# Depthwise-convolution taps taken off GpSimd, a new fold of the layer norm's squares, and a last residual add shared by four engines

## The reference

```python
def conformer_conv(h, w_pw1, b_pw1, w_dw, b_dw, ln_g, ln_b, w_pw2, b_pw2):
    u = h @ w_pw1 + b_pw1
    a, gate = jnp.split(u, 2, axis=-1)
    u = a * jax.nn.sigmoid(gate)
    u = lax.conv_general_dilated(u, w_dw[:, None, :], ...) + b_dw
    u = jax.nn.silu(layer_norm(u, ln_g, ln_b))  
    return u @ w_pw2 + b_pw2
```

## Time and profile before

| | us |
|---|---|
| median of 3 runs (lowest to highest) | 1835.67 (1832.31 to 1838.24) |
| the profiled execution's own time | 1825.88 |
| its span in the trace | 1824.1 |
| busy: TensorE, VectorE, ScalarE, GpSimd | 1770.6, 992.7, 632.3, 232.5 |

### The profile page before, as it was taken

One profiled execution on the slowest core, in us unless ns is written; L12 is line 12 of the kernel. 1 busy time (PEld: TensorE's weight loads), 2 busy tenths in 40 slices (PEclk: granted clock), 3 DMA queues, 4 the chain that ended last, 5 costly groups with the idle time before them and its releaser, 6 DMA issues.

```text
span 1824.1 us, 22032 instructions
## 1 busy us (share of the span) xinstructions
PE 1770.6 (97%) x8104; PEld 1438.0 (79%) x8104; DVE 992.7 (54%) x1299; ACT 632.3 (35%) x928; POOL 232.5 (13%) x200
## 2 busy tenths in 40 slices
PE   6999999999999999999999999999999999999997
PEld 5777888888888887867888888877767788888885
DVE  4566346663665389974743244336675564234423
ACT  4345234441344353343422123234264433113220
POOL 2100021110111122311110011000000111002111
PEclk9999899999999999989999999999999999999998
DMA  5212023333223222312133223321210223323221
GB/s 183 83 47 71 22 94 100 99 117 96 91 92 104 70 93 83 106 66 89 63 104 103 92 93 102 95 92 48 95 43 1 93 81 103 95 92 101 92 81 46
DMA packets 43844, 156.05 MB, mean 86 GB/s; under 512 B 4864, under 2 KB 4992, under 8 KB 43776
## 3 DMA queue, kind: packets, MB, share of 16 engines
q1 hardware_dynamic: 43632, 154.19, 26.3%
q10 hardware_dynamic: 144, 0.92, 0.1%
HBM read 153.00 MB, written 2.10 MB: 85 GB/s over the span
## 4 chain that ended last, share of the span: by engine, by line
PE 85%; DVE 11%; ACT 2%; issue 1%; POOL 0%; DMA 0%; POOLq 0%; SPq 0%; ACTq 0%; DVEq 0%
PE bank L1037 25%; PE bank L1038 24%; PE bank L1039 24%; DVE cv L1998 4%; DVE w_lo L1683 2%; PE bank L1172 1%; PE bank L1178 1%; PE bank L1173 1%; PE bank L1078 1%; PE bank L1248 1%; PE bank L1114 1%; PE bank L1277 1%; PE bank L1624 1%; ACT w_hi L622 1%; PE bank L1104 0%
## 5 line engine op out<-in xcount | busy, mean ns | idle before, releaser
L1683 DVE TENSOR_TENSOR w_lo<-w_raw,w_hi 128x1024 fp32r<-128x1024 f32 x283 | 367.9, 1301 | 319.3 <-ACT w_hi L622 196.5
L1037 PE MATMUL bank<-a_hi,w_hi 128*128 128x512 f32 x1156 | 460.4, 398 | 22.7 <-DVE w_lo L1683 20.1
L1038 PE MATMUL bank<-a_lo,w_hi 128*128 128x512 f32 x1156 | 455.4, 394 | 0.0
L1039 PE MATMUL bank<-a_hi,w_lo 128*128 128x512 f32 x1156 | 453.5, 392 | 0.0
L1037 PEld LDWEIGHTS bank<-a_hi,w_hi 128*128 128x128 f32 x1156 | 218.6, 189 | 77.5 <-issue 15.3
L1037 PE MATMUL bank<-g_hi,w_hi 128*128 128x512 f32 x688 | 270.1, 393 | 0.0
L1038 PE MATMUL bank<-g_lo,w_hi 128*128 128x512 f32 x688 | 270.0, 392 | 0.0
L1039 PE MATMUL bank<-g_hi,w_lo 128*128 128x512 f32 x688 | 267.7, 389 | 0.0
L1039 PEld LDWEIGHTS bank<-a_hi,w_lo 128*128 128x128 f32 x1156 | 218.4, 189 | 49.3
L1038 PEld LDWEIGHTS bank<-a_lo,w_hi 128*128 128x128 f32 x1156 | 218.8, 189 | 46.0 <-issue 1.0
L622 ACT ACTIVATE w_hi<-w_raw 128x1024 fp32r<-128x1024 f32 x167 | 173.9, 1049 | 174.1 <-PE bank L1039 168.9
(11 more groups left out here) (290 smaller groups left out, 2042.8 us busy)
## 6 DMA issues: line engine op xcount, KB each, us to landing
w_raw<-in_stream SPq DMA_DIRECT2D x283, 512.0 KB, 3.5
h<-in_xT SPq DMA_DIRECT2D x8, 256.0 KB, 6.7
out<-h SPq DMA_DIRECT2D x8, 256.0 KB, 2.0
cst_b<-in_consts SPq DMA_DIRECT2D x1, 896.0 KB, 9.7
cst_b<-in_consts ACTq DMA_DIRECT2D x1, 896.0 KB, 4.6
cols<-in_vectors SPq DMA_DIRECT2D x1, 289.0 KB, 2.8
cst<-in_consts SPq DMA_DIRECT2D x1, 257.0 KB, 8.3
w_al<-in_w_alpha SPq DMA_DIRECT2D x1, 128.0 KB, 9.9
```

The costliest lines, as they stand in the source:

```text
L1037: pe.matmul(out, w0, x0, start=start, stop=False, skip_group_check=loose)
L1038: pe.matmul(out, w0, x1, start=False, stop=False, skip_group_check=loose)
L1039: return pe.matmul(out, w1, x0, start=False, stop=stop, skip_group_check=loose)
L1683: dve.tensor_tensor(w_lo[slot][:, :], w_raw[slot][:, :], f(w_hi[slot][:, :]), ALU.subtract)\
```

## The change

`TAPS_PE` becomes `[12, 12, 12, 20]` and `TAPS_POOL` goes away, with its ScalarE products and its GpSimd adds; VectorE has 18, 18, 18 and 10 taps per tile, 128 in all. The tap units become 3, 3, 3 and 5. `w_hi` and `w_lo` of `pw2`'s units 2 and 3 are made ahead of the mean, behind the last tap addition. The layer norm's squares go into `m`; GpSimd adds two pairs, VectorE folds the other four tiles to one, and TensorE sums three tiles instead of four. The idle matmuls are laid differently: two before the mean instead of four, four behind it instead of two, others of 192, 512 and 256 columns between and behind the sums, and one instead of four behind the spread. In the last residual add VectorE does tiles 0 and 7, GpSimd 1, 3 and 5, and for tiles 2, 4 and 6 TensorE adds `h` and `m` in a bank by identity matmuls and ScalarE copies the bank to `h`; `h`'s own part is loaded into the banks in place of idle matmuls and behind the spread.

```diff
-TAPS_PE = [12, 12, 16, 16]
-TAPS_POOL = [2, 2, 3, 4]
+TAPS_PE = [12, 12, 12, 20]
...
+        def out_bank(k):
+            return bank[{2: 2, 4: 3, 6: 5}[k]]
...
@block.sync
             for k in range(KD):
-                sp.wait_ge(out_added if k % 2 else out_ready, k // 2 + 1)
+                if k in (2, 4, 6):
+                    sp.wait_ge(out_copied, k // 2)
+                elif k in (1, 3, 5):
+                    sp.wait_ge(out_added, k // 2 + 1)
+                else:
+                    sp.wait_ge(out_ready, 1 if k == 0 else 2)
                 sp.dma_start(outT[k * P:(k + 1) * P, :], T(h, k)).then_inc(out_stored, 16)
...
@block.gpsimd
-            def add_taps(k):
-                pool.wait_ge(last_tap, k + 1)
-                for j in range(TAPS_POOL[k // 2]):
-                    no = pool_taps(k) + j
-                    pool.wait_ge(tap_product, no + 1)
-                    if j:
-                        pool.wait_ge(pool_tap, no)
-                    pool.tensor_tensor(T(cv, k), T(cv, k), sq_buf[no % 2], ALU.add).then_inc(pool_tap, 1)
...
-                add_taps(2 * p)
-                add_taps(2 * p + 1)
...
-            for p in range(KD // 2):
+            for p in range(2):
                 pool.wait_ge(sq_ready, SQ0["ln_var"] + 2 * p + 2)
-                pool.tensor_tensor(ln_sq_buf(2 * p), ln_sq_buf(2 * p), ln_sq_buf(2 * p + 1), ALU.add)\
-                    .then_inc(sum_added, 1)
+                pool.tensor_tensor(T(m, 2 * p), T(m, 2 * p), T(m, 2 * p + 1), ALU.add).then_inc(ln_pairs, 1)
...
-            for k in range(1, KD, 2):
-                pool.wait_ge(out_scaled, (k + 1) // 2)
+            for k in (1, 3, 5):
+                pool.wait_ge(out_scaled, k)
                 pool.tensor_tensor(T(h, k), T(h, k), T(m, k), ALU.add).then_inc(out_added, 1)
...
@block.scalar
-                for j in range(TAPS_POOL[k // 2]):
-                    tap = CONV_W - 2 - j
-                    no = pool_taps(k) + j
-                    if no >= 2:
-                        act.wait_ge(pool_tap, no - 1)
-                    act.activation(sq_buf[no % 2], u_pad[:, k * UW + tap:k * UW + tap + SEQ], ACT.Copy,
-                                   scale=col("w_dw", k * CONV_W + tap)).then_inc(tap_product, 1)
...
+            w_hi_of(UNIT0["pw2"] + AHEAD, (UNIT0["pw2"] + AHEAD) % RING)
             load_sqrt(STAT_NO["ln_var"])
             act.wait_ge(mean_done, 1)
             for k in range(KD):
                 act.wait_ge(cen_ready, k + 1)
-                act.activation(ln_sq_buf(k), T(cv, k), ACT.Square, scale=float(D) ** -0.5).then_inc(sq_ready, 1)
-            w_hi_of(UNIT0["pw2"] + AHEAD, (UNIT0["pw2"] + AHEAD) % RING)
+                act.activation(T(m, k), T(cv, k), ACT.Square, scale=float(D) ** -0.5).then_inc(sq_ready, 1)
...
             feed_forward(1)
+            for k in (2, 4, 6):
+                act.wait_ge(out_summed, k // 2)
+                act.activation(T(h, k), out_bank(k)[:, :], ACT.Copy).then_inc(out_copied, 1)
...
@block.tensor
+            def h_part(k, c0, c1):
+                pe.matmul(out_bank(k)[:, c0:c1], cst[:, IDENT:IDENT + P], T(h, k)[:, c0:c1], start=(c0 == 0), stop=False,
+                          skip_group_check=True)
...
@@ in stat
-                if "post" in name:
+                if name == "ffpost1":
+                    pe.wait_ge(out_read, TILE0["ff2b1"])
+                    h_part(2, 0, 384)
+                elif "post" in name:
                     run_idle(6, 1, 384)
...
@@ in spread
+                if name == "ffpost1":
+                    h_part(4, 0, 384)
+                elif "post" in name:
                     run_idle(6, 1, 384)
...
             pe.wait_ge(out_read, TILE0["pw2"])
-            run_idle(0, 4)
+            run_idle(0, 2)
             pe.wait_ge(mean_add, KD - 2)
             pe.matmul(bank[4][:, :], cst[:, MEAN:MEAN + P], ssum[:, :], start=True, stop=False)
-            pe.wait_ge(cv_ready, KD)
-            pe.matmul(bank[4][:, :], cst[:, MEAN:MEAN + P], T(cv, KD - 2), start=False, stop=False)
-            pe.matmul(bank[4][:, :], cst[:, MEAN:MEAN + P], T(cv, KD - 1), start=False, stop=True)\
-                .then_inc(mean_done, 1)
+            for k in (KD - 2, KD - 1):
+                pe.wait_ge(cv_ready, k + 1)
+                last = pe.matmul(bank[4][:, :], cst[:, MEAN:MEAN + P], T(cv, k), start=False, stop=(k == KD - 1))
+            last.then_inc(mean_done, 1)
             run_idle(0, 2)
-            for p in range(KD // 2):
-                if p:
-                    run_idle(0, 1, P)
-                pe.wait_ge(sum_added, ADD0["ln_var"] + p + 1)
...
+            run_idle(0, 2)
...
+            pe.wait_ge(ln_pairs, 1)
+            ln_sum(0, True, False)
+            run_idle(0, 1, 192)
+            pe.wait_ge(ln_pairs, 2)
+            ln_sum(2, False, False)
+            run_idle(0, 1)
+            pe.wait_ge(ln_folded, 1)
+            ln_sum(4, False, True).then_inc(stat_done, 1)
+            run_idle(0, 1, 256)
             spread("ln_var")
-            run_idle(0, 4)
+            run_idle(0, 1)
             tiles("pw2", 8, a_hi, a_lo, "conv")
...
             feed_forward(1)
+            h_part(2, 384, SEQ)
+            h_part(4, 384, SEQ)
+            h_part(6, 0, SEQ)
+            run_idle(6, 1)
+            for k in (2, 4, 6):
+                pe.wait_ge(out_scaled, k)
+                pe.matmul(out_bank(k)[:, :], cst[:, IDENT:IDENT + P], T(m, k), start=False, stop=True,
+                          skip_group_check=True).then_inc(out_summed, 1)
...
@block.vector
-                return CONV_W - 1 - TAPS_POOL[p] - TAPS_PE[p]
+                return CONV_W - 1 - TAPS_PE[p]
...
-                        dve.wait_ge(pool_tap, pool_taps(c + 1))
+                        dve.wait_ge(last_tap, c + 1)
...
             add_pe_taps(KD // 2 - 1)
+            lo_ahead(UNIT0["pw2"] - 1)
+            lo_ahead(UNIT0["pw2"])
             dve.wait_ge(mean_done, 1)
             for k in range(KD):
                 dve.tensor_tensor(T(cv, k), T(cv, k), bank[4][:, :], ALU.subtract).then_inc(cen_ready, 1)
-            lo_ahead(UNIT0["pw2"])
+            for k, other in ((4, 5), (6, 7), (4, 6)):
+                dve.wait_ge(sq_ready, SQ0["ln_var"] + max(k, other) + 1)
+                fold = dve.tensor_tensor(T(m, k), T(m, k), T(m, other), ALU.add)
...
-            post_norm("ffpost1", "ffpost", 8, None)
+            take_r("ffpost1")
+            dve.wait_ge(spread_done, STAT_NO["ffpost1"] + 1)
+            for k in range(KD):
+                scale = dve.scalar_tensor_tensor(T(m, k), T(m, k), col("ffpost", 8 + k), bank[4][:, :],
+                                                 ALU.mult, ALU.mult)
+                if k in (0, KD - 1):
+                    link(scale)
+                    dve.tensor_tensor(T(h, k), T(h, k), T(m, k), ALU.add).then_inc(out_ready, 1)
+                else:
+                    scale.then_inc(out_scaled, 1)
```

More of the change, by code:

```diff
@@ L110 @@
     _s = _s + _n
-    if _name not in IN_M:
-        _a += max(_n - 2, 0) if _name != "ln_var" else KD // 2
+    if _name not in IN_M and _name != "ln_var":
+        _a += max(_n - 2, 0)
 R_NO = {name: i for i, name in enumerate(n for n, _ in STATS if "post" not in n and n != "ln_var")}
@@ L366, in program @@
         ln_silu = sem("ln_silu")
+        ln_pairs = sem("ln_pairs")
+        ln_folded = sem("ln_folded")
         h_ready = sem("h_ready")
@@ L444, in conv_step @@
             return first, taps
-        def pool_taps(c):
-            return sum(TAPS_POOL[k // 2] for k in range(c))
         def conv_bank(c):
@@ L2012, in _ @@
                 for q, n in enumerate(units):
-                    if n > UNIT0["pw1"]:
+                    if UNIT0["pw1"] < n < UNIT0["pw2"] - 1:
                         lo_ahead(n)
@@ L2038, in _ @@
                 dve.tensor_tensor(T(cv, k), T(cv, k), bank[4][:, :], ALU.subtract).then_inc(cen_ready, 1)
-            lo_ahead(UNIT0["pw2"])
+            for k, other in ((4, 5), (6, 7), (4, 6)):
+                dve.wait_ge(sq_ready, SQ0["ln_var"] + max(k, other) + 1)
+                fold = dve.tensor_tensor(T(m, k), T(m, k), T(m, other), ALU.add)
+                if other == 6:
+                    fold.then_inc(ln_folded, 1)
+                else:
+                    link(fold)
             take_r("ln_var")
@@ L2054, in _, with post_norm @@
                 dve.tensor_scalar(T(m, k), bank[k % 4][:, :], col("b_pw2", k), None, ALU.add).then_inc(out_read, 1)
-            def post_norm(stat, gain, g0, h0=None, split=None, next_gain=None, ng0=0, product=None):
+            def post_norm(stat, gain, g0, split, next_gain, ng0, product=None):
                 take_r(stat)
@@ L2065, in post_norm @@
                                                      ALU.mult, ALU.mult)
-                    if not split and k % 2:
-                        scale.then_inc(out_scaled, 1)
-                        continue
                     link(scale)
```

(9 more changed lines are left out.)

22 lines of the change are left out of this document (10 added, 12 removed).

## The result

The changed kernel's median is 1814.74 us (1813.4 to 1816.22, four runs) beside 1833.99 us for the kernel before (four runs): a ratio of 0.9895, 95% interval 0.9871 to 0.9919. So the kernel is 0.9 to 1.0% faster, 16 to 19 us. Forecast were 16.0 us (0.9913).

The account below looks back on a forecast made before the run. It took TensorE to bound the kernel, winnable only in waits, idle matmuls and low clock; gains of 7.0, 2.9, 2.9 and 3.2 us made 16.0: 1809.9 us profiled, 1819.7 timed, range 1814 to 1827.

Parts of the forecast that it names:

- Taps: Convolution: VectorE's end of taps moves from 794.5 to 785.8 us, TensorE's last unit from 790.6 to 786.2.
- The stretch: Convolution: 18 removed GpSimd adds lay beside VectorE's taps and what follows, costing it 1.04 us each, 18.7 in all.
- the two stalls and the low clock: Convolution: TensorE's two waits for w_lo, 2.7 us, and the half clock behind them, 1.7, together 4.4.
- Mean: Layer norm: the mean's last matmul ends (time M) at 790.9 us instead of 797.85, gain 7.0.
- Variance: Layer norm: scaling starts 9.8 us behind M, the end of the mean's last matmul, instead of 12.7; gain 2.9.
- The first rival: Layer norm: the clock falls all the same, costing 3.4 to 5.1 us, time 1823 to 1825; chance 20%.
- A clock of 0.5 around 795 us: Layer norm: a granted clock this low there was named as a sign that the forecast is wrong.
- First matmul of pw2: Behind the norm: one idle matmul instead of four frees TensorE in time for the first product, gain taken as 2.9 us.
- The end: Last residual add: the span ends 10.4 us behind T, the last norm's first scale, instead of 13.6; gain 3.2.
- VectorE starving TensorE: Convolution: TensorE still waits once for VectorE, so 4.4 us of wait and low clock stay, 1824 us; chance 12%.
- The folds: Variance: VectorE's folds meet GpSimd's second pair and lose 0.5 us, 1820.2, or up to 1.27, 1821; chance 5%.
- The slower side: Convolution: the stretch isn't GpSimd's doing and VectorE becomes the bound, 8.8 us slower, 1844.5 us; chance 3%.

Follow-up runs that it names:

- e7: The changed kernel with 22 GpSimd adds on unused spare tiles put back at the old tap adds' places: 1839.7 us, one run.
- e3: The kernel before with only the change's end part, the last residual add shared by four engines: ratio 1.0006 to the kernel before.
- e12: The changed kernel without idle matmuls before the mean, one w_lo moved into VectorE's wait for the spread, 192 idle columns widened to 448: 1811.97 us, ratio 0.9902.
- e5: The changed kernel again, unedited, against more runs of the kernel before: 1814.37 us beside 1831.0, ratio 0.9914.
- the first profile: The first profiled execution of the changed kernel, unedited: 1813.4 us, span 1811.6 us.
- e2: The kernel before with only the change's layer norm part: ratio 0.9983 to the kernel before.
- e9: The changed kernel with TensorE's old tap shares, TAPS_PE [12, 12, 16, 16]: ratio 0.9940 to the kernel before.
- e10: The changed kernel with four idle matmuls instead of one behind the layer norm's spread: ratio 0.9942 to the kernel before.
- e6: The changed kernel with the old end, VectorE adding even tiles and GpSimd odd ones: 1818.4 us, ratio 0.9932 to the kernel before.
- e8: The changed kernel with 22 spare GpSimd memsets, which read nothing, at the old tap adds' places: 1815.1 us, one run.
- e1: The kernel before with only the change's convolution part, 128 taps on VectorE and none on GpSimd: ratio 0.9975 to the kernel before.
- e4: The kernel before again, unedited: profiled execution 1829.74 us, median of runs 1830.97 us, ratio 1.0009 to the kernel before.

## Why the prediction was right, point by point

*What bounds the stage.* Right: VectorE's stretched taps held up w_lo, and with GpSimd's tap adds gone nothing waits for it. With adds on spare tiles back in their place (e7) it waits again.

*Taps.* Forecast for VectorE's end of taps 785.8, measured 785.3; the sum's terms stand nearly. The stretch was put at 18.7. In e7 it is 18.7 again, but that is not the same sum tap for tap: in the kernel before 14 of the 18 adds lie beside taps and stretch them by 1.04 each, the others mostly stretch u_lo and w_lo. The 1.2 us that VectorE idled for ScalarE's w_hi between 654 and 794.5 and that went away too were not counted. The early start of the first step was taken at 3.5 and came to 3.4 (650.97 for 654.33). Forecast for TensorE's last unit 786.2, measured 785.7: the two stalls and the low clock were worth 4.9, not 4.4; by e3, the low clock's 1.7 of it could have been missing before.

*Mean.* Forecast 790.9, measured 790.2. The two idle matmuls were counted as on the path. e12 shows that 1.5 of their 1.7 us are, once the second w_lo is out of the way as well.

*Variance.* Forecast M + 9.8 at full clock: 10.0 in e5, 11.8 in the first profile. The first rival, given 20%, is what happened in that profile: 6.8 us of low clock from 796.8. With the same idle work ahead of the spread the clock was low in that profile, e2, e7, e9 and e10, and up in e5, e6 and e8. Five of eight is far from 20%: the chance of this rival was the forecast's weakest number. Its price was overrated, 3.4 to 5.1 against 1.9 (216.9 less 215.0), since the low stretch lay mostly on sums, idle work and the spread and was over when pw2 began. The argument that the last norm has the same pattern and keeps its clock did not carry over. A clock of 0.5 around 795 us was named as a sign of being wrong, and the first profile shows one from 796.9 on; what it cost was small enough to leave the forecast's total in place. The prediction had set against itself the sentence of the Trainium skill, in TensorE: Matmul & The Clock Gate, Part 1, that the throttled state is the default and activity releases it. Whether the idle matmuls taken away would have held the clock no run here shows: the old arrangement lost it too (e1, e3, e4), and in e10 it fell before the three that were put back.

*First matmul of pw2.* Forecast 1.5 behind scaling, measured 1.55.

*The end.* Forecast T + 10.4, measured 10.8: the copies came as forecast (7.2 for 7.3), and the last four tiles crowded by 0.7, less than the 1.0 allowed (2.7 from the last issue to the end instead of 2.1). What was left out is SyncE's own time: its last issue was done at T + 8.1, not T + 7.4. The kernel before had shown it, for 11.1 and 2.0 make 13.1 and not the 13.6 that the forecast started from. Gain 2.7 for 3.2.

*The sum.* 16.0 forecast; 16.4 by the distances in e5, 15.7 by its timed ratio, 19.3 between the medians of the first comparison. That the total came out within half a us owes something to luck: the mean gained 0.7 to 0.8 more than forecast and the end 0.5 less, and in the first profile the variance gained 2.0 less. The forecast's absolute level, 1819.7, is 5.0 too high because it rested on a median of three runs of the kernel before at 1835.7; 35 runs of it on a later occasion had 1830.5, and its own second profile 1829.7.

*The other rivals.* VectorE starving TensorE: no wait for w_lo. The folds did not meet GpSimd's second pair; they take 0.69 us each. The slower side needs the stretch to stay, and e7 made it stay: 1839.7 us, slower than the kernel before (1831.0), as that rival had it, though 5.6 us of that are the slower pace told of below.

## What to carry to other kernels

Before work is given to GpSimd beside a busy VectorE, compare what it saves with what it takes: here a tap cost VectorE 0.66 us to do and 1.04 us to have done. Two engines that meet at the end of a stage should be balanced by their last step, not by their totals; moving four taps per tile was worth 3.0 us at the mean. And idle matmuls put in to hold the clock belong off the path: count them there like any other instruction.
